# Neighbourhood attention's scores: one exact multiplication replaced by three in the rounded format

## The reference, cut to what matters

```
def neighborhood_attention(h, w_qkv, rpb, w_o):      # S = 512 tokens, a grid of 8 rows x 64
    qkv = (h @ w_qkv).reshape(B, rows, GRID_W, 3, NA_HEADS, NA_HEAD_DIM)   # 16 heads of 64
    q = qkv[0] * (NA_HEAD_DIM ** -0.5)
    ...
        s = jnp.einsum('bhcd,bhicjd->bhcij', q_r, k_win).astype(jnp.float32)
        s = s + bias[None].astype(jnp.float32)
        a = jax.nn.softmax(...)                       # over a window of 8 x 16 keys
        return jnp.einsum('bhcij,bhicjd->bhcd', a.astype(v.dtype), v_win)
    ...
    return o @ w_o
# first_block:  x = x + rms_norm(m, g[1])   with m the attention's result and x the input
```

## Time and profile before

| | |
|---|---|
| median of 3 runs | 2231.64 us |
| the profiled execution's own time | 2231.41 us |
| its span, first to last instruction | 2229.6 us |
| PE busy over the span | 2165.4 us, 97% |
| DVE, ACT busy over the span | 57%, 40% |
| mean granted TensorE clock | 0.995 of full speed |

### The profile page before, as it was taken

How to read it: one execution, slowest core, us unless ns; L and a number is a source line. 1 busy time by engine, 2 the same in 40 slices (tenths; PEclk the granted TensorE clock), 3 DMA queues, 4 the chain that set the end, 5 groups by cost and what they waited for, 6 DMA issues and landing times. The chain is left out here.

```text
span 2229.6 us, 35501 instructions
## 1 busy us (share of the span) xinstructions
PE 2165.4 (97%) x14014; PEld 1719.0 (77%) x14014; DVE 1280.8 (57%) x1653; ACT 896.0 (40%) x1405; POOL 119.8 (5%) x96
## 2 busy tenths in 40 slices
PE   8999999999999999999999999999898899999999
PEld 6787788888876677778888887777787566888887
DVE  6564576663377777566665347686456476333333
ACT  4444532222364566642222244655222444323221
POOL 0000011110000000001111000000233000000000
PEclk9999999999999999999999999999999999999999
DMA  7331233333323222123233331322000111333321
GB/s 254 104 112 59 76 114 95 100 97 95 95 78 111 82 72 67 52 72 113 94 94 104 95 94 57 102 76 85 3 4 4 47 39 58 113 94 97 101 94 66
DMA packets 52933, 187.65 MB, mean 84 GB/s; under 512 B 5840, under 2 KB 6096, under 8 KB 52688
## 3 DMA queue, kind: packets, MB, share of 16 engines
q1 hardware_dynamic: 52528, 185.39, 26.6%
q10 hardware_dynamic: 288, 0.59, 0.1%
HBM read 183.86 MB, written 2.10 MB: 83 GB/s over the span
## 5 line engine op out<-in xcount | busy, mean ns | idle before, releaser
L297 PE MATMUL l_banks<-l_r_hi,l_w_hi 128*128 128x512 f32 x1440 | 573.9, 399 | 2.9 <-DVE l_r_lo L1748 2.3
L299 PE MATMUL l_banks<-l_r_hi,l_w_lo 128*128 128x512 f32 x1440 | 561.2, 390 | 0.0
L298 PE MATMUL l_banks<-l_r_lo,l_w_hi 128*128 128x512 f32 x1440 | 561.1, 390 | 0.0
L282 DVE TENSOR_TENSOR l_w_lo<-ring,l_w_hi 128x1024 fp32r<-128x1024 f32 x216 | 299.0, 1386 | 106.7 <-ACT l_w_hi L276 102.9
L276 ACT ACTIVATE l_w_hi<-ring 128x1024 fp32r<-128x1024 f32 x216 | 227.0, 1055 | 290.6 <-PE l_banks L299 285.9
L297 PEld LDWEIGHTS l_banks<-l_r_hi,l_w_hi 128*128 128x128 f32 x1440 | 270.6, 188 | 72.6 <-issue 8.9
L298 PEld LDWEIGHTS l_banks<-l_r_lo,l_w_hi 128*128 128x128 f32 x1440 | 270.8, 188 | 57.0 <-issue 3.6
L299 PEld LDWEIGHTS l_banks<-l_r_hi,l_w_lo 128*128 128x128 f32 x1440 | 270.5, 188 | 57.3
L297 PE MATMUL ff_banks<-ff_r_hi,ff_w_hi 128*128 128x512 f32 x512 | 200.0, 391 | 0.0
L299 PE MATMUL ff_banks<-ff_r_hi,ff_w_lo 128*128 128x512 f32 x512 | 199.2, 389 | 0.0
L298 PE MATMUL ff_banks<-ff_r_lo,ff_w_hi 128*128 128x512 f32 x512 | 199.2, 389 | 0.0
(11 more groups left out here) (505 smaller groups left out, 3221.5 us busy)
## 6 DMA issues: line engine op xcount, KB each, us to landing
ring<-weights SPq DMA_DIRECT2D x315, 512.0 KB, 3.6
na_bias<-window_bias SPq DMA_DIRECT2D x16, 512.0 KB, 5.4
da_rel<-t_rel SPq DMA_DIRECT2D x8, 448.0 KB, 4.3
X<-xT SPq DMA_DIRECT2D x8, 256.0 KB, 5.6
outT<-X SPq DMA_DIRECT2D x8, 256.0 KB, 2.1
const<-consts SPq DMA_DIRECT2D x1, 1312.0 KB, 11.2
l_pt<-pT SPq DMA_DIRECT2D x2, 512.0 KB, 4.7
kr<-mla_consts SPq DMA_DIRECT2D x1, 512.5 KB, 6.0
```

What stands on the lines that cost most here:

```text
L282: dve.tensor_tensor(self.w_lo[:, c % self.slots, :], k.ring[:, g % RING, :], self.w_hi[:, c % self.slots, :].bitcast(F32), ALU.subtract).t ...
L297: pe.matmul(psum, hi, self.hi(rhs_slot), start=start, stop=False)
L298: pe.matmul(psum, hi, self.lo(rhs_slot), start=False, stop=False)
L299: return pe.matmul(psum, lo, self.hi(rhs_slot), start=False, stop=stop)
```

## The change

Queries and keys of the scores get the same treatment as the projections' operands.

- ACT writes the rounded queries and keys (`round_queries`, `round_keys`, 8 of each, 128x512) into a new tile `qk_hi`. It has no room of its own: it is laid over the first four tiles of X.
- DVE writes the rests (`queries_lo`, `keys_lo`, 8 of each, 128x512). `ql` and `kl` are laid over `qb` and `kb` and have their shape, so each rest replaces its source in place.
- PE makes each score from three calls in the rounded format instead of one in fp32: 12 calls a part instead of 4, 192 in all instead of 64. Each shows as one load and one matmul. The two heads of a block still follow each other directly.
- X's first four tiles are loaded again by SP, once the last scores are made (`scored` at 16), ahead of the output projection's refills. The tail waits for them before it adds to X.

```
+        with ExitStack() as under:
+            self.qk_hi = under.enter_context(nc.sbuf_tensor("qk_hi", [P, 4, S], F32R))
         self.X = self.sb("X", [P, DT, S])
...
+    qh, kh = k.qk_hi[:, 0:2, :], k.qk_hi[:, 2:4, :]
+    with ExitStack() as under:
+        ql, kl = (under.enter_context(k.nc.sbuf_tensor(f"na_{n}", [P, 2, S], F32R)) for n in ("ql", "kl"))
     qb, kb = (sb(n, [P, 2, S]) for n in ("qb", "kb"))
...
+        sp.wait_ge(scored, 2 * PAIRS)
+        for j in range(4):
+            sp.dma_start(k.X[:, j, :], k.dram["xT"][j * P:j * P + P, :]).then_inc(k.x_loaded[j], 16)
...
         def scores(t, part):
             if part == 0:
-                pe.wait_ge(evacuated, AT[1, t] + 1)
+                pe.wait_ge(qk_split, 2 * t + 2)
...
             for b in range(2):
-                for h in range(2):
-                    mm = pe.matmul(s_ps[:, h, b, :], qb[half(h), t % 2, (2 * part + b) * P:(2 * part + b + 1) * P],
-                                   window(kb[half(h), t % 2, :], 2 * part + b), start=True, stop=True)
+                queries = slice((2 * part + b) * P, (2 * part + b + 1) * P)
+                for n, (q, key) in enumerate(((qh, kh), (qh, kl), (ql, kh))):
+                    for h in range(2):
+                        mm = pe.matmul(s_ps[:, h, b, :], q[half(h), t % 2, queries], window(key[half(h), t % 2, :], 2 * part + b),
+                                       start=n == 0, stop=n == 2)
             mm.then_inc(scored, 1)
...
+        def queries_lo(t):
+            dve.wait_ge(qk_rounded, 2 * t + 1)
+            dve.tensor_tensor(ql[:, t % 2, :], qb[:, t % 2, :], qh[:, t % 2, :].bitcast(F32), ALU.subtract).then_inc(qk_split, 1)
+        def keys_lo(t):
+            dve.wait_ge(qk_rounded, 2 * t + 2)
+            dve.tensor_tensor(kl[:, t % 2, :], kb[:, t % 2, :], kh[:, t % 2, :].bitcast(F32), ALU.subtract).then_inc(qk_split, 1)
...
+            queries_lo(t)
             evacuate((1, t))
...
             if t >= 2:
                 normalise(t - 1)
+            keys_lo(t)
...
+        def round_queries(t):
+            act.wait_ge(evacuated, AT[0, t] + 1)
+            act.activation(qh[:, t % 2, :], qb[:, t % 2, :], ACT.Copy).then_inc(qk_rounded, 1)
+        def round_keys(t):
+            act.wait_ge(evacuated, AT[1, t] + 1)
+            act.activation(kh[:, t % 2, :], kb[:, t % 2, :], ACT.Copy).then_inc(qk_rounded, 1)
...
             round_ahead((0, t))
+            round_queries(t)
...
             round_ahead((1, t))
+            round_keys(t)
...
+                    if norm == 0 and j < 4 and x_back:
+                        dve.wait_ge(k.x_loaded[j], x_back)
```

More of the change, by code:

```diff
@@ L769, in neighborhood @@
     (squared, gathered, summed, lned, rstd_done, evacuated, scored, added, maxed, exped, inverted, normed, turned, t_free,
-     weighed, o_out, out_split) = (st.sem(f"na_{n}") for n in (
+     weighed, o_out, out_split, qk_rounded, qk_split) = (st.sem(f"na_{n}") for n in (
          "squared", "gathered", "summed", "lned", "rstd_done", "evacuated", "scored", "added", "maxed", "exped", "inverted",
-         "normed", "turned", "t_free", "weighed", "o_out", "out_split"))
+         "normed", "turned", "t_free", "weighed", "o_out", "out_split", "qk_rounded", "qk_split"))
     bias_loaded = [st.sem(f"na_bias_loaded{n}") for n in range(4)]
@@ L1482, in layer_tail @@
     gate_bank = [1, 2, 3, 5, 6, 7, 4, 5]
+    x_back = (32, 0)[layer]
     gains = [(f"g{layer}1", f"g{layer}2"), (f"g{layer}3", f"g{layer}4")]
```

## The result

The changed kernel takes 2234.88 us (median of 20 runs, 2232.08 to 2239.64), the kernel before 2230.53 us in the same series (20 runs, 2229.36 to 2233.04). The ratio is 1.0019, with a 95% interval from 1.0012 to 1.0025: 2.7 to 5.6 us slower, about 4.2. The forecast was +2.45 with a range up to +9; direction and mechanism held, the size came out short by one term. The two profiled executions, against which the sum was made, differ by 3.4 us (2234.83 and 2231.41). The forecast time, 2234.1 us, lies closer to the measured 2234.88 than the forecast difference lies to the measured one; that part is luck, since the three runs that it started from had a median 1.1 us above that of the 20.

A forecast was written before the change was run, and what follows sets the result against it. PE's own work and stalls were taken as the bound. Scores' parts -2.08, first scores +2.33, keys' rounding +0.50 and clock +1.7 sum to +2.45 us, 2234.1 us on the median; 8-in-10 range 2229.5 to 2240.8.

The forecast's parts named there:

- The scores' part: PE's scores: a part takes 0.91 us instead of 1.07, gaining 0.16; thirteen parts give -2.08 us.
- The bad ends of this term: Slower rivals for a part's scores: 1.39 us if loads aren't hidden (chance 0.12), 1.65 us if heads run apart (0.10).
- The first scores: PE's wait before the first scores: DVE's added work delays them to 34.56, +2.33 us, stall from 1.46 to 3.79 us.
- The gain lost in later stalls: PE's stalls before scores(1, 1) and the values' transposition: three of sixteen parts give nothing back.
- The keys' rounding ahead of the copy: ACT's row in pair 2: rounding keys before the copy of transposed weights that PE waits for costs +0.50 us.
- The clock: Behind the first scores' stall: PE's clock falls to half, costing 1.7 us, two chances in three.
- The reload: X's tiles and the held refills after the last scores: there by 205, cover of 20 and 55 us, costing nothing.

The follow-up runs named there:

- experiment 6: Changed kernel with only the pass of rounded queries by rounded keys; rests still made and waited for; 0.9992 of the kernel before.
- experiment 8: Changed kernel with both heads' score matmuls on the first 64 partitions, head 1's scores left out; 1.0072 of the kernel before.
- Experiment 1: Changed kernel with the first pair's scaling, rounding and rests ahead of two weight chunks on ACT and DVE; 0.9992 of the kernel before.
- experiment 2: Changed kernel with four unused fp32 matmuls of constants on PE in front of the first scores; 1.0006 of the kernel before.
- experiment 4: Changed kernel with the first scores moved on PE into the middle of the chunk of k(1); 0.9992 of the kernel before.
- Experiment 9: Changed kernel, first pair's rounding and rests before weight chunks, first scores mid-chunk, pair 2's keys' rounding behind the transposed weights' copy; 0.9987 of the kernel before.
- experiment 7: Changed kernel with all eight tiles of X loaded again in place of four, the tail waiting for all; 1.0017 of the kernel before.
- experiment 3: Changed kernel with three matmuls of one head, then three of the other, in PE's sequence; 1.0011 of the kernel before.
- experiment 5: Kernel before with its fp32 scores, plus the change's roundings, rests and wait, and all eight tiles of X reloaded; 1.0030 of the kernel before.

## Why the prediction was right, and where it was short

**The scores' part, right.** Taken 0.91 us, measured 0.92; step 0.12 taken and measured. Twelve later parts gave 1.79 us. The bad ends of this term are both shown to be off: the loads of one pair hide behind the running one (experiment 6: 0.12 a step with its load), and the heads do run side by side (experiment 8 gives the price if they didn't). The Trainium skill's rule on loads (TensorE: Matmul & The Clock Gate, Part 3, the mechanism), that they overlap a running matmul only on other rows, is not what these rows show: steps on the same rows start 0.12 us apart with a new load each, and in experiment 8 the loads at 112.17 start while matmuls on the same rows run (111.94 to 112.45). The same place of the page also has a second case, loads into a background weight buffer, and these rows would fit that one.

**The first scores, right.** 34.56 taken, 34.62 measured, and the stall 3.79 in both. It could be added up from starts because DVE never waits in that row: ACT's roundings fell into the gaps, as worked out. Experiment 1 shows that it was the order and not the amount of work.

**The gain lost in later stalls, right.** The second stall grew by 0.29 us for two parts' gain of 0.3; the lag of 3.76 us stayed the same across it.

**The keys' rounding ahead of the copy, right in kind.** The third stall was 1.85 us, 2.1 where the clock was at 1.00 (experiments 1, 2 and 4), against 1.47: 0.50 for the rounding and 0.15 of a part. Experiment 9 took the rounding out of it and the stall fell to 1.6.

**The clock, the term that was mis-sized.** I took one fall behind the first stall, at 1.7 us. What the stall cost in clock can be read from two stretches of each profile, the one behind the first scores and the one around the two later stalls (columns as in the earlier trace rows). The changed kernel:

```profile
34.60:42.00 7.40, 7.38 (x33) 6.00 (x34) 3.50 (x5) 0.63 (x1) 0.00 (x0) 0.77 0.50 143
57.00:75.00 18.00, 15.26 (x79) 12.77 (x80) 11.76 (x16) 9.69 (x23) 0.00 (x0) 0.91 0.33 114
```

and the one with twice the reload (experiment 7):

```profile
34.60:42.00 7.40, 7.34 (x28) 5.95 (x29) 3.62 (x5) 0.63 (x1) 0.00 (x0) 0.60 0.44 146
57.00:75.00 18.00, 14.32 (x82) 11.53 (x82) 12.90 (x17) 10.17 (x23) 0.00 (x0) 1.00 0.40 137
```

Length times what is missing to 1.00, from PE's return on: 7.4 x 0.23 + 18 x 0.09 = 3.3 us in the first, two falls; 7.4 x 0.40 = 3.0 us in the second, one fall that lasts about twice as long. All six kernels with the stall of 3.8 us (the changed one and experiments 3 and 5 to 8) read like one or the other, between 2.5 and 3.3 us. The six without it lose nothing in these stretches, but for experiment 4, whose one fall behind the later waits costs 1.6. Experiment 2 leaves the timing as it is and fills the wait, and the loss is gone: its weighing of pair 6 starts 2.6 us earlier. So the clock costs about 3 us (2.5 to 3.3) where the sum had 1.7. Put in, the forecast of +2.45 becomes +3.8, beside the measured 4.2 and the 3.4 between the two profiled executions.

That the first fall came was not well founded either, though it came in all six kernels with this stall. I had sorted stalls by length from one trace: 1.87 us fell, 1.86 us did not. Other traces undo that sorting. The stall at 905 us comes back in the changed kernel with the same 1.87 us, and the clock stays at 1.00; the one of 1.86 us at 1872 us is followed by a fall in experiments 6 and 9.

What stays open is the second fall. It came behind waits of 1.6 us (changed kernel), 2.1 us (experiment 3) and 2.0 us (experiment 5), and the fall of experiment 4 behind one of 2.1 us, while the same waits in experiments 1, 2 and 7 brought none. The three kernels with the short first fall had a second one, the three with the long first fall had none; with one profile of each kernel I can't say how often it comes, nor whether the first fall has a part in it. The wider spread of the changed kernel's runs (7.6 us, against 3.7 before) goes with the clock: its six fastest runs (2232.1 to 2233.9 us) have a mean granted clock of 0.995 to 0.996, its two slowest (2239.4 and 2239.6) 0.991 and 0.992. Where in those runs the clock fell isn't on record.

**The reload, right.** It starts at 201.17, the refills behind it are issued from 203.29, and ACT takes the first chunk at 230.02 without waiting; twice the reload costs nothing (experiment 7).

## What to carry to other kernels

When a producer gets a second step (round, subtract) in sequences written out by hand, look at what stands between the steps at the one place where the consumer already waits: here a weight split that nobody needed yet stood there, and with the two rests and the falls of the clock behind the stall it turned a gain of 2 us into a loss of 4. A stall of PE costs more than its length, because PE may come back at half its clock (3.8 us of stall cost about 3 more); fill it or move other work into it. And a gain ahead of a stall that is tied to another engine's chain is worth nothing until that chain is shortened.

## What the hardware did that I had not expected

- Matmuls for different halves of the array's rows are not held to the program's order. With three of one head followed by three of the other they still started in pairs, 0.12 us a step (experiment 3); on one half the same twelve take 0.24 us a pair (experiment 8).
- The granted clock fell to 0.50 behind a wait of 1.57 us in one execution and stayed at 1.00 behind 1.57 and 1.59 us in others (experiments 1 and 2), so the length of a wait alone doesn't decide it. The stall at 905 us of the earlier trace rows says the same: 1.87 us again in the changed kernel, no fall, and the four matmuls behind it last 1.13 us instead of 1.81.

```profile
908.90 1.13 PE L1239 MATMUL l_banks<-da_kb,da_qb 64*128 64x512 f32 x4 [1.87 <-DVE H L1338]
```

- Behind one and the same stall of 3.8 us the low stretch was of two lengths: 3.4 us in the changed kernel, from 35.0 to 38.4 (mean 0.77 over the 7.4 us above), and 6.8 us with twice the reload, from 33.7 to 40.6 (mean 0.60). In the changed kernel and experiments 3 and 5 it began within 0.4 us of PE's return and was short; in experiments 6 to 8 it began 0.7 to 1.6 us before PE's return and was long. Here are two stretches of the one with twice the reload, whose PE came back at 34.66 (columns as in the earlier trace rows):

```profile
33.00:34.00 1.00, 0.00 (x0) 0.00 (x0) 1.00 (x2) 1.00 (x2) 0.00 (x0) 0.86 0.64 254
40.00:41.00 1.00, 1.00 (x5) 0.81 (x4) 0.00 (x0) 0.00 (x0) 0.00 (x0) 0.72 0.00 0
```

- A fall needs no wait of PE. In the kernel before the clock fell at 1557.3 us, and PE had not waited in the 17 us ahead of it; its last work were 3.7 us of small matmuls, 32 of them, each on 6 partitions. These are the first of them, and the stretch of the fall:

```profile
1553.54 1.95 PE L2015 MATMUL in_side<-const,pi 6*128 6x6 f32 x16
1557.00:1561.00 4.00, 4.00 (x13) 3.19 (x13) 0.00 (x0) 0.00 (x0) 0.00 (x0) 0.57 0.00 0
```
